# Ends of five stages interleaved with the starts of the next: transposes inside matmul groups, the embedding product moved ahead, the last down tiles token by token

## What is computed

```python
def rms_norm(x, g):
    xf = x.astype(jnp.float32)
    y = xf * lax.rsqrt(jnp.mean(xf * xf, axis=-1, keepdims=True) + EPS)
    return (y * g.astype(jnp.float32)).astype(x.dtype)

def conv_ffn(h, w_up, conv_w, conv_b, w_down):
    a, b = jnp.split(h @ w_up, 2, axis=-1)
    a = causal_dwconv(a, conv_w, conv_b)
    return (jax.nn.gelu(a) * b) @ w_down

...
    for i in range(DEPTH):
        j = i // 2
        if i % 2 == 0:
            h = h + ab_mixer(rms_norm(h, ab_norm_g[j]), ab_w_in[j], ab_conv_w[j], ab_conv_b[j],
...
        else:
            h = h + nsa_mixer(rms_norm(h, nsa_norm_g[j]), nsa_w_in[j], nsa_q_norm_g[j], nsa_k_norm_g[j],
...
        h = h + conv_ffn(rms_norm(h, ffn_norm_g[i]), ffn_w_up[i], ffn_conv_w[i], ffn_conv_b[i], ffn_w_down[i])
        e = rms_norm(p[i] @ ple_w[i], ple_norm_g[i])
        gate = jax.nn.sigmoid(rms_norm(h, ple_gate_norm_g[i]) @ ple_w_gate[i])
        h = h + gate * e
```

## Time and profile before

| | us |
|---|---|
| median of 3 runs | 2412.09 (2407.84 to 2416.21) |
| the profiled execution, its own time | 2415.46 |
| its span, first to last instruction | 2413.6 |
| TensorE busy | 2065.9 |
| VectorE busy | 708.6 |
| ScalarE busy | 335.5 |
| mean granted TensorE clock | 0.924 of full speed |

### The profile page before, as it was taken

One profiled execution on the slowest core, in us unless ns is written; L12 is line 12 of the kernel. 1 busy time (PEld: TensorE's weight loads), 2 busy tenths in 40 slices (PEclk: granted clock), 3 DMA queues, 4 the chain that ended last, 5 costly groups with the idle time before them and its releaser, 6 DMA issues.

```text
span 2413.6 us, 20625 instructions
## 1 busy us (share of the span) xinstructions
PE 2065.9 (86%) x8515; PEld 1097.1 (45%) x8515; DVE 708.6 (29%) x1344; ACT 335.5 (14%) x719; POOL 67.1 (3%) x81
## 2 busy tenths in 40 slices
PE   7989999898999998999697787876599687887785
PEld 4547766455577664444433333332255433333231
DVE  1236664325366553022300000000664300000001
ACT  1221101115210012000110000000234100000001
POOL 0000000001000000000000000000100100000000
PEclk9979999998999998999699989898699699999998
DMA  8526677254266673111599999999310799999995
GB/s 310 183 70 228 237 247 250 79 171 141 70 244 242 245 252 120 37 70 64 220 428 427 427 428 427 427 428 398 123 70 32 285 427 427 427 427 428 427 427 226
DMA packets 154846, 639.57 MB, mean 265 GB/s; under 512 B 16784, under 2 KB 67664, under 8 KB 130048
## 3 DMA queue, kind: packets, MB, share of 16 engines
q1 hardware_dynamic: 135328, 596.04, 62.3%
q0 software_dynamic: 10112, 25.31, 2.9%
q10 hardware_dynamic: 9312, 16.88, 1.8%
HBM read 623.38 MB, written 25.30 MB: 269 GB/s over the span
## 4 chain that ended last, share of the span: by engine, by line
PE 69%; DMA 18%; DVE 5%; issue 5%; ACT 3%; SPq 0%; POOL 0%; ACTq 0%; DVEq 0%; POOLq 0%
PE psum L474 17%; PE psum L1891 13%; PE psum L896 13%; DMA ring<-in_w 8%; PE psum L884 6%; PE psum L1909 6%; DMA normed_t<-in_w 6%; PE psum L1426 3%; DMA arena<-in_w 3%; DVE normed_t L449 1%; PE psum L1557 1%; ACT arena L1241 1%; DMA arena<-expert_outputs,row_of_choice 1%; PE psum L977 1%; PE psum L1565 1%
## 5 line engine op out<-in xcount | busy, mean ns | idle before, releaser
L1891 PE MATMUL psum<-ring,arena 128*64 128x512 f32 x1280 | 388.5, 667 | 109.8 <-issue 107.9
L474 PE MATMUL psum<-ring,normed_t 128*128 128x512 f32 (+1 forms) x864 | 354.3, 573 | 2.9 <-DMA ring<-in_ab_w_in 1.2
L896 PE MATMUL psum<-normed_t,ring 128*128 128x256 f32 x1408 | 310.4, 383 | 2.7 <-DVE normed_t L449 2.7
L1891 PEld LDWEIGHTS psum<-ring,arena 128*64 128x64 f32 x1280 | 129.4, 153 | 359.1 <-issue 359.1
L896 PEld LDWEIGHTS psum<-normed_t,ring 128*128 128x128 f32 x1408 | 270.7, 192 | 44.1 <-issue 3.8
L474 PEld LDWEIGHTS psum<-ring,normed_t 128*128 128x128 f32 x864 | 163.1, 200 | 188.7 <-issue 185.9
L2166 DVE TENSOR_TENSOR scaled<-scaled,psum 128x512 f32<-128x512 f32 x32 | 22.0, 687 | 631.3 <-PE psum L1891 631.3
L816 DVE SCALAR_TENSOR_TENSOR arena<-ring,silu_c,arena 128x1024 f32<-128x1024 f32 x168 | 204.5, 1278 | 0.0
L1909 PE MATMUL psum<-ring,consts 128*64 128x512 f32 x640 | 173.2, 600 | 26.1 <-DMA ring<-in_w 11.9
L884 PE MATMUL psum<-ring,arena 128*128 128x512 f32 x352 | 154.3, 596 | 0.0
L1891 PE MATMUL psum<-arena 128*64 128x512 f32 x512 | 123.0, 636 | 32.8 <-issue 32.8
(11 more groups left out here) (383 smaller groups left out, 1792.3 us busy)
## 6 DMA issues: line engine op xcount, KB each, us to landing
ring<-in_w SPq DMA_DIRECT2D x120, 2048.0 KB, 28.9
arena<-in_w SPq DMA_DIRECT2D x48, 2048.0 KB, 29.3
ring<-in_w_mod SPq DMA_DIRECT2D x24, 2048.0 KB, 8.3
normed_t<-in_w SPq DMA_DIRECT2D x24, 2048.0 KB, 33.1
ring<-in_ffn_w_up SPq DMA_DIRECT2D x44, 1024.0 KB, 10.0
ring<-in_ffn_w_down SPq DMA_DIRECT2D x10, 2048.0 KB, 9.2
expert_outputs<-consts ACTq DMA_DIRECT2D x64, 256.0 KB, 10.4
ring<-in_ab_w_in SPq DMA_DIRECT2D x6, 2048.0 KB, 21.3
```

What stands on the lines that cost most here:

```text
L474: m = te.eng.matmul(PS[:, bank, 0:n], src[:, k0 + k, P * t:P * t + P], w[:, k, :], start=(k == 0), stop=(k == kc - 1))
L896: m = pe.matmul(PS[:, b, 256 * hf:256 * hf + 256], w[:, hf, k, P * cc:P * cc + P], HT[:, k, 0:T], start=(k == 0), stop=(k == KC - 1))
L1891: m = pe.matmul(PS[64 * h:64 * h + 64, 2 + q, :], XT[:, c % 2, k, 64 * h:64 * h + 64], w[h][:, k, :], start=k == 0, stop=k == KC - 1)
```

## The change

Six edits, all of them of order:

1. In the last out-projection of ab and nsa, the four transposes of `p` (`emb_turn`) come ahead of the last group but one, and the 8 transposes of tile 0 for the feed-forward norm come inside the last group (ahead of its sixth chunk in ab, of its first in nsa).
2. The feed-forward stage begins with half of the embedding product (tile 0), the transposes of tile 1, and the other half. ScalarE and VectorE do the norm of the embedding there too. Its result `EE` lies in dead constants until ple.
3. `down4` is cut: its first two chunks run as before, its last two with the two of `down5` in `down_last`, where tile 0 gets all four chunks before tile 1 gets any. The transposes of tile 0 for the gate come ahead of the last chunk of tile 1.
4. The gate products are ordered tile by tile, with transposes between them: of the stage's own tile 1, of both context tiles (ple1), and of tile 0 of the next stage.
5. nsa begins with the products q instead of c, and em with `em.a` of tile 2; the transposes of tile 1 follow the first group. The banks of em are exchanged.
6. The weights of the embedding product stand ahead of `ffn.up0` in `stream`, and q0 and q1 ahead of c.

The number of matmuls and transposes, the bytes loaded and the expert stages stay as they are. ScalarE has two more loads of its table in each ple stage. In all other places the diff writes `wait(eng, ...)` out as `eng.wait_ge(...)`, the same instruction.

```diff
+        def norm_bank(name, t, hf):
+            return 2 * (t % 2) + hf + (4 if name == "n.mix0" and t >= 2 else 0)
...
+        def rows(te, name, t, bank, reader, n=512, c0=0, src=None, tag=None, last=False, kc=KC, k0=0, within=(-1, None)):
...
+                if k == within[0]:
+                    within[1]()
                 m = te.eng.matmul(PS[:, bank, 0:n], src[:, k0 + k, P * t:P * t + P], w[:, k, :],
                                   start=(k == 0), stop=(k == kc - 1))
...
-                    rows(te, f"ab.out{n}", t, 2 * n + t, ("dve", f"ab.res{n}{t}"), src=YH, last=t == 1)
+                    rows(te, f"ab.out{n}", t, 2 * n + t, ("dve", f"ab.res{n}{t}"), src=YH, last=t == 1,
+                         within={(1, 0): (0, lambda: emb_turn(te, 0)), (1, 1): (5, lambda: norm_pe(te, "n.ffn0", (0,)))}.get((n, t), (-1, None)))
...
+                    if (n, t) != (1, 1):
+                        dv.wait_ge(sems["pe"], upto("pe", f"ab.out{n}.t{t}"))
                     xr = X[:, t, 512 * n:512 * n + 512]
+                    if (n, t) == (1, 1):
+                        norm_columns(dv, p, "n.ffn0", (0,), lambda t: g_ffn[0])
+                        dv.wait_ge(sems["pe"], upto("pe", "ab.out1.t1"))
                     p.step(dv.tensor_tensor(xr, xr, PS[:, 2 * n + t, :], ALU.add), f"ab.res{n}{t}")
                     if n and on("ffn0"):
...
-            norm_pe(te, f"n.ffn{i}", (0, 1))
-            wait(pe, "dve", f"n.ffn{i}.ht1")
-
-            def down(j):
+            emb_product(te, i, 0)
+            norm_pe(te, f"n.ffn{i}", (1,))
+            emb_product(te, i, 1)
+            pe.wait_ge(sems["dve"], upto("dve", f"n.ffn{i}.ht0"))
+            pe.wait_ge(sems["dve"], upto("dve", f"n.ffn{i}.ht1"))
+
+            def down(j, nk=4):
                 w = te.weights(f"ffn{i}.down{j}").rearrange("p (c n) -> p c n", n=D)
-                nk = min(4, FC - 4 * j)
                 for cc in range(nk):
                     c = 4 * j + cc
-                    wait(pe, "dve", f"ffn{i}.g{c}")
+                    pe.wait_ge(sems["dve"], upto("dve", f"ffn{i}.g{c}"))
                     for t in range(2):
                         for n in range(2):
                             if c == 0:
                                 te.take(4 + 2 * n + t, "dve", f"ffn{i}.res{n}{t}")
                             m = pe.matmul(PS[:, 4 + 2 * n + t, :], GT[:, c, P * t:P * t + P], w[:, cc, 512 * n:512 * n + 512],
                                           start=(c == 0), stop=(c == FC - 1))
-                p.step(m, f"ffn{i}.down{j}.used")
+                p.step(m, *([f"ffn{i}.down{j}.used"] if nk == 4 else []))
+
+            def down_last():
+                w = [te.weights(f"ffn{i}.down{j}")[:, 0:nk * D].rearrange("p (c n) -> p c n", n=D)[:, nk - 2:nk] for j, nk in ((4, 4), (5, 2))]
+                for t in range(2):
+                    for cc in range(4):
+                        c = 18 + cc
+                        pe.wait_ge(sems["dve"], upto("dve", f"ffn{i}.g{c}"))
+                        if (t, cc) == (1, 3):
+                            norm_pe(te, f"n.plg{i}", (0,))
+                        for n in range(2):
+                            m = pe.matmul(PS[:, 4 + 2 * n + t, :], GT[:, c, P * t:P * t + P], w[cc // 2][:, cc % 2, 512 * n:512 * n + 512],
+                                          start=False, stop=(c == FC - 1))
+                    p.step(m, f"ffn{i}.y{t}", *([f"ffn{i}.down4.used", f"ffn{i}.down5.used"] if t else []))
 
             for j in range(FC // 2):
                 w = te.weights(f"ffn{i}.up{j}").rearrange("p (h k n) -> p h k n", h=2, k=8)
...
                 if on("mod") and j in MOD_SUM_AFTER:
                     mod_sum(te, i, MOD_SUM_AFTER[j])
                 if j >= 2 and j % 2 == 0:
-                    down(j // 2 - 1)
+                    down(j // 2 - 1, 4 if j < 10 else 2)
             if on("mod"):
                 mod_sum(te, i, 5)
-            down(FC // 4)
+            down_last()
...
-            norm_act(ac, p, f"n.ffn{i}", (0, 1), after)
+            norm_table(ac, p)
+            ac.wait_ge(sems["dve"], upto("dve", after(0)))
+            norm_act_tile(ac, p, f"n.ffn{i}", 0)
+            ac.wait_ge(sems["pe"], upto("pe", f"ple{i}.ptr"))
+            p.step(ac.activation(PT, PS[:, 4 - 4 * i, :].rearrange("p (k t) -> p k t", k=2), ACT.Copy), f"ple{i}.pt")
+            ac.wait_ge(sems["dve"], upto("dve", after(1)))
+            norm_act_tile(ac, p, f"n.ffn{i}", 1)
+            for t in range(2):
+                ac.wait_ge(sems["pe"], upto("pe", f"ple{i}.e.t{t}"))
+                p.settle()
+                p.step(ac.activation(EJ.rearrange("p (b n) -> p b n", b=2), PS[:, 4 + 2 * t:6 + 2 * t, :], ACT.Square,
+                                     accum_out=SM[:, 890 + t:891 + t]), f"ple{i}.sq{t}")
+                ac.wait_ge(sems["dve"], upto("dve", f"ple{i}.inv{t}"))
...
-            wait(dv, "pe", f"ffn{i}.down{FC // 4}.used")
-            for n in range(2):
-                for t in range(2):
+            for t in range(2):
+                if t:
+                    norm_columns(dv, p, f"n.plg{i}", (0,), lambda t: g_plg[i])
+                dv.wait_ge(sems["pe"], upto("pe", f"ffn{i}.y{t}"))
+                for n in range(2):
                     xr = X[:, t, 512 * n:512 * n + 512]
                     p.step(dv.tensor_tensor(xr, xr, PS[:, 4 + 2 * n + t, :], ALU.add), f"ffn{i}.res{n}{t}")
-                    if n and on(f"ple{i}"):
-                        norm_scale(dv, p, f"n.plg{i}", t)
-
-
-        EE = Z[:, 0:2048].rearrange("p (t n) -> p t n", t=2)
...
+        def emb_turn(te, i):
+            pe, p = te.eng, te.p
+            ptok = te.weights(f"ple{i}.w")[:, 2048:2560].rearrange("p (t n) -> p t n", t=2)
+            te.take(4 - 4 * i, "act", f"ple{i}.pt")
+            for t in range(2):
+                for k in range(2):
+                    m = pe.transpose(PS[:, 4 - 4 * i, 256 * k + P * t:256 * k + P * t + P], ptok[:, t, P * k:P * k + P], ident)
+            p.step(m, f"ple{i}.ptr")
+
+        def emb_product(te, i, t):
+            pe, p = te.eng, te.p
+            pe.wait_ge(sems["act"], upto("act", f"ple{i}.pt"))
+            w2 = te.weights(f"ple{i}.w")[:, 0:2048].rearrange("p (k n) -> p k n", k=2)
+            for n in range(2):
+                te.take(4 + 2 * t + n, "dve", f"ple{i}.e{t}")
+                for k in range(2):
+                    m = pe.matmul(PS[:, 4 + 2 * t + n, :], PT[:, k, P * t:P * t + P], w2[:, k, 512 * n:512 * n + 512],
+                                  start=(k == 0), stop=(k == 1))
+            p.step(m, f"ple{i}.e.t{t}", *([f"ple{i}.w.used"] if t == 1 else []))
+
+        PLE_NEXT = ("n.nsa", "n.mix0")
 
         def ple_pe(te, i):
+            gate = lambda n, t: rows(te, f"ple{i}.gate{n}", t, 2 * n + t, ("act", f"ple{i}.sg{n}{t}"), last=t == 1)
+            gate(0, 0)
+            norm_pe(te, f"n.plg{i}", (1,))
+            gate(1, 0)
+            if i == 1:
+                norm_pe(te, "n.mix0", (2, 3))
+                te.norm = f"n.plg{i}"
+            gate(0, 1)
+            norm_pe(te, PLE_NEXT[i], (0,))
+            te.norm = f"n.plg{i}"
+            gate(1, 1)
+            te.norm = PLE_NEXT[i]
...
+        def ple_act(ac, p, i, after):
...
+            norm_table(ac, p)
+            for t in range(2):
+                ac.wait_ge(sems["dve"], upto("dve", after(t)))
+                norm_act_tile(ac, p, f"n.plg{i}", t)
+            for t in range(2):
+                if i == 1 and t == 0:
+                    ac.wait_ge(ctx_loaded, 16)
+                    for u in (2, 3):
+                        ac.wait_ge(sems["pe"], upto("pe", f"n.plg1.tr{u - 2}1"))
+                        norm_act_tile(ac, p, "n.mix0", u)
                 for n in range(2):
+                    ac.wait_ge(sems["pe"], upto("pe", f"ple{i}.gate{n}.t{t}"))
                     p.step(ac.activation(SG[:, t, 512 * n:512 * n + 512], PS[:, 2 * n + t, :], ACT.Sigmoid), f"ple{i}.sg{n}{t}")
+                norm_table(ac, p)
+                ac.wait_ge(sems["dve"], upto("dve", f"ple{i}.res1{t}"))
+                if i == 1:
+                    ac.wait_ge(sems["pe"], upto("pe", f"n.mix0.tr{t + 2}1"))
+                else:
+                    ac.wait_ge(sems["pe"], upto("pe", f"n.plg0.tr{t}1"))
+                norm_act_tile(ac, p, PLE_NEXT[i], t)
...
+            norm_columns(dv, p, f"n.plg{i}", (1,), lambda t: g_plg[i])
+            if i == 1:
+                dv.wait_ge(ctx_loaded, 16)
+                for t in (2, 3):
+                    norm_scale(dv, p, "n.mix0", t)
+            for t in range(2):
+                for n in range(2):
+                    if (t, n) == (1, 1):
+                        if i == 0:
+                            norm_columns(dv, p, "n.nsa", (0,), lambda t: g_nsa)
+                        else:
+                            norm_columns(dv, p, "n.mix0", (0,), lambda t: MODC[:, 0, 0, 1, :], lambda t: MODC[:, 0, 0, 0, :])
```

(25 more changed lines are left out.)

579 lines of the change are left out of this document (274 added, 305 removed).

## The result

The changed kernel took 2377.98 us in the median of four runs (2374.91 to 2381.10), the kernel before 2414.15 beside it: ratio 0.9856, 95% interval 0.9843 to 0.9870. In a later set of runs the same two took 2371.27 and 2414.83: ratio 0.9818 (0.9804 to 0.9833). The forecast was 2372, the range 2364 to 2388: both medians lie in it. As a ratio to the kernel before the forecast is 0.983, between the two measured ones. The profiled execution took 2381.10 (span 2379.3).

What follows compares the result with a forecast made beforehand. TensorE was taken to bound the kernel up to about 1150 us, expert weights after. Joints of 71.8 us less 28.9 of work and 3.0 of waits give 39.9 off; against 2412.09 the forecast was 2372, range 2364 to 2388.

Steps and rivals of the forecast that it cites:

- The joints before and the work that stays: Six joints between stages, ab to em: 62.2 us plus 9.6 of clock before; 28.9 us of transposes and embedding products stay.
- The clock, given back in full: Behind joints into ffn0, nsa, ffn1 and em: 1.9, 2.1, 3.2 and 2.4 us lost to low clock, all recovered.
- The waits that stay: TensorE waits left at the joints after the change: 3.0 us in sum, at ple0 gates, nsa, ple1 gates and em.
- em tile 0: In ple1, ahead of tile 0's transposes for em, VectorE is late: a wait of 1.1 us, and 0.35 for the bank.
- The margins of 0.9 and 0.1 in ab and ffn: Tile 0's norm in ab ready 0.9 us before TensorE needs it, tile 1's in ffn 0.1 us before: no wait.
- The bank waits: At both gates and into nsa TensorE waits 0.3 to 0.4 us each for a bank; 0.35 once in each layer.
- The same 40 us: Sign in the next profile: em's first group some 40 us earlier, and the first expert earlier by the same.
- Late fillers: Rival at the joints: thin margins fail or handovers add up, low clock returns at two; 14 us more, 2386; chance 0.14.
- loads late: Rival: slots held longer delay q1 or em's c by a landing at two joints, 2x10.7 us; 2395; chance 0.03.
- swallowed: Rival: expert weights arrive no earlier, so the gain before 1150 us becomes a longer wait for them; 2407; chance 0.04.
- The pause behind a table load: Rival in the ple stages: a pause after ScalarE's table load delays sigmoids; 2.3 us more, 2374; chance 0.04.
- Slower by sustained clock: Rival: TensorE running some 900 us almost without pause lowers its clock; over 2412, 2422 at 100 us; chance 0.03.

Runs made afterwards that it cites:

- k2: The changed kernel with the joint from ple1 to em undone: all four tiles' norms and transposes behind the gate products; 2392.71 us, ratio 0.9909 to the kernel before.
- u2: The changed kernel with the embedding product put back between the first and second gate product; 2387.83 us, ratio 0.9885 to the kernel before.
- u3: The changed kernel with the last down products of both token tiles side by side again, tile 0's transposes behind them; 2396.04 us, ratio 0.9924 to the kernel before.
- k1: The kernel before, with products that nobody reads put into the waits of four of the six joints; 2403.99 us, ratio 0.9959 to the kernel before.
- k4: The changed kernel with the context tiles' column instructions in ple1 moved behind tile 0's second addition and scaling; 2373.35 us, ratio 0.9833 to the kernel before.
- u1: The changed kernel with tile 0's eight transposes behind the last out-projection group, ahead of the embedding product, in both layers; 2373.68 us, ratio 0.9832 to the kernel before.

## Why the prediction was right

- **What bounds.** Right: TensorE at the joints, up to 1100 us. k2, u2 and u3 lengthen a joint and the end moves with it, within the scatter of the expert stages.
- **The joints before and the work that stays.** Right: 39.9 us forecast, 41.1 and 42.3 measured in two executions. No two errors cancel between the layers: the prediction's own terms give 16.7 us as far as nsa and 23.2 behind it, measured 17.1 and 24.0.
- **The clock, given back in full.** Right: both up blocks are at 41.44. k1 shows that TensorE's standing still is what costs it, for three of the four places; ahead of em it stays open.
- **The waits that stay.** em tile 0: 1.20 for VectorE, against 1.1, and k4 takes away its cause. The margins of 0.9 and 0.1 in ab and ffn held. The bank waits show as 0.39 to 0.46 us of issue.
- **Mis-sized: what lies outside the joints.** The sum put it at nothing. In the profiled execution it was 6.8 us lost: its own time was 2381.1 where the text said 2375.6. The second profiled execution of the same kernel took 2375.28. No part of it is tied to the change. How near a median comes to 2372 is therefore partly luck (2378 in one set, 2371 in the other); the 41.1 of the joints is not.
- **A sign that came out otherwise.** The same 40 us were to show at the first expert; there it was 35.9, since the way to it took the long form in this execution.
- **The rivals.** Late fillers, loads late and swallowed didn't come: no joint has a new wait but the one named, and the gain at em's columns (38.9 us) is there at the second layer's first q product too (1723.99 and 1685.08). (The text's price for late loads, 2395, is 2 us too high by its own terms: 2372 and 2x10.7 make 2393.) The pause behind a table load didn't come: in ple1 the load starts at 904.94 and takes 1.28, and the sigmoid starts at 906.24. The drain that the Trainium skill adds there (ScalarE: Activation LUTs, What ACT_TABLE_LOAD costs) is not in this trace either. Slower by sustained clock: 437.9 us at 1.00 say no.
- **Not foreseen.** The parts do not add. Undone one at a time, three of them cost 15.9, 21.4 and 15.3 us of joint, 52.6 in all, more than the 41.1 that the whole gave, and u1 costs nothing. Each filler and each reordering is worth what the others leave bare.
- **Not tested alone.** The joint into nsa, whose stretch went from 99.91 to 90.81, and the new order of the loads (edit 6) were never undone by themselves; what they are worth is known from the stretch alone.

## What to carry to other kernels

Price a joint as the distance from the last product to the first, take off the work that must stay, then count which tile is ready when; that sum held to 1.2 and 2.4 us in 40. Split the last products by token tile first, then look for work to put behind the last tile: the filler alone was worth nothing, everything but the filler 25 of 41 us. Once TensorE's waits are gone, look at the small transfers: in the joints next to the expert weights they set the time here, and the write that started earlier, beside those loads, took more than twice as long.

## What the runs showed of the hardware

- Behind waits of 2.40 and 1.36 us the up block was slow (192 records in 43.36 us); with these waits two thirds filled it was not (41.71). Behind a single wait of 1.20 us in ple1 32 records took 13.90 us, behind one of 1.60 at the same place in u2 15.21.
- In a stretch with many short waits the granted clock is not the same from run to run (0.86, 0.88, 0.90 in nsa's attention), and with it the stretch varies by 2.6 us under unchanged code. The 64 router records take 8.2 to 8.6 us or 10.6 to 10.8.
- A 512 KB write of GpSimd's queue lands in 6.6 us, or in 15.9 beside loads of 2 MB from another queue, and in 7.4 when these are held; a gather in 4.4, or in 7.9 beside them.
- ScalarE's table load takes 1.28 us, and where the next activation's input is ready it starts 0.01 to 0.02 us behind the load.
